# A hybrid decoder step on one Trainium2 core: the mixer one tile at a time, and decode attention alone in later slots

## The chip, the cores and the metric

The kernel runs on one core of one Trainium2 chip. The metric is the device time of one execution in microseconds; before the change it was 2877.15 us, the median of three runs (2869.53 to 2877.79). Smaller is better.

## The reference, cut to what matters

One layer is computed for two groups of tokens with the same weights: a prompt of 512 tokens (four tiles of 128, numbered 0 to 3) and a sample of 8 sequences with 4 new tokens each (32 rows, tile 4, called PT), which see 4096 past tokens in a paged cache. All is float32.

```
h = rms_norm(x); proj = h @ w_in                 # 1024 -> 13 blocks of 512 columns
o_a = stick_breaking_attention(qa, ka, va)       # prompt: keys up to the own tile; sample: 32 pages of 128 keys per sequence
o_b = retention(qb, kb, vb, state)               # prompt: state carried from tile to tile; sample: 8 states loaded and stored
y_b = (rms_norm(o_b) * silu(gb)) @ w_b_up
merged = sigmoid(ga) * (o_a @ w_a_up) + sigmoid(gb_pre) * y_b
x = x + merged @ w_out
h2 = rms_norm(x)                                 # experts: 8 heads, top 16 of 16384 for each token and head
x = x + sum_k softmax(top)_k * gelu(u_tab[e_k] . h2) * v_tab[e_k]
y = x + sigmoid(rms_norm(x) @ w_ple_gate) * (p_emb @ w_ple)
```

Each tile thus reads all of w_in, w_a_up, w_b_up, w_out and the expert query weights, and each head of a tile gathers 16 rows of u_tab and 16 of v_tab (4 KB each) for each of its 128 tokens.

## The kernel before, in words

**Two streams of work.** The expert part is cut into 34 slots, one for each head of each prompt tile, and two for the sample (32 rows by 4 heads fill a slot). A slot is 16 gathers from u_tab into 16 ring buffers, 16 products on VectorE (L1917, in `dve_dots`), the gelu weights (`dve_weights`, whose third instruction is L1930, so that its start marks the slot), 16 gathers from v_tab into the same buffers, and 64 matmuls on TensorE (L1998, in `pe_weigh`); slot i+2's top-k runs two slots ahead. GpSimd issues all gathers (L2009) and, once a block of slots, the h2 rows of the next tile (L2006). A buffer is gathered into for slot i+1 only when `pe_weigh` has read it for slot i.

The rest (the mixer) runs in the background of the slots. It is cut into groups of tiles and stages: N norm, Q the projections qa, ka, va, A prompt attention, D decode attention, R projections and rotation for retention, T retention, G the output gate, M the merge, O the output projection and h2, K the expert queries and scores; then L, the last gate with the embeddings, for each tile. `when(q, stage, unit)` gives each step of each stage a place on the axis of slots, by fixed costs in `STAGE_COST`; each engine has a written-out order in which `Background.until(s)` emits the mixer steps that are due before the part of the slot that comes next. So TensorE, VectorE and ScalarE each execute one list in order, in which slot work and mixer steps alternate, and a wait of one holds up the other.

**Groups before.** `GROUPS = [[0], [1, PT], [2, 3]]`. Group 0 runs ahead of the slots; group 1, with the sample and decode attention, is placed at slots -0.5 to 5.9; group 2 at 6.02 to 15.9. From slot 16 on only the gates (L) remain. The slots of the sample are 16 and 17, between tile 1 and tile 2.

**Weights.** `load_weights` (L439) loads halves of 1024 KB on SyncE's queue into three buffers, in the order of `W_ORDER`: 44 halves for each group (26 of w_in, 4 of w_b_up, 2 of w_a_up, 4 of w_out, 8 of peer_w_q). Each half is used by all tiles of the group. `project` (L453) is 8 matmuls of 128x512 outputs for a tile, `sample_parts` (L463) the same for the 32 rows of the sample in four column groups, which ScalarE copies (`keep_parts`) and TensorE adds (L478).

**Decode attention.** 64 units, four pages of keys and four of values each (256 KB a page). SyncE reads the page number (L2030) and issues the page's DMA (L2035) in the order of `load_cache`; keys and values have two buffers of four pages each. TensorE turns the keys (L749), ScalarE copies them (L1211), TensorE makes the scores (L760), and, some units later, weighs the values (L812). In group 1 it stands between A and R, so all of R to K of tile 1 and of the sample comes after it.

**Retention of the sample** (L919, L927, in T): for each of the 8 sequences a state of 512 KB is loaded, used, updated on VectorE (L1712) and stored, with two buffers. SyncE waits for each update and each store in its order (L2069, L2072).

**Start of the slots.** GpSimd waits for group 0's K on all engines, then loads the h2 rows and waits for the index of slots 0 (`pool.wait_ge(idx_put, 2)`) before the first gather; VectorE begins the first top-k when the mixer's steps up to -0.9 are done.

## Time and profile before

| | before |
|---|---|
| median of three runs | 2877.15 us |
| profiled execution | 2866.99 us |
| its span | 2865.0 us |
| TensorE busy | 1831.4 us, 64% |
| VectorE busy | 1312.3 us, 46% |
| GpSimd busy | 1227.7 us, 43% |
| ScalarE busy | 493.1 us, 17% |
| moved by DMA | 896.09 MB, mean 313 GB/s |
| mean granted TensorE clock | 0.79 |

Busy shares are means over stages that have different limits. The share of the 16 DMA engines is a mean of the time that packets took; where two queues both have work it can come out a little over 1, and its highest value in a long stretch (1.03) is read as full. GB/s times microseconds gives the bytes of a stretch. The span leaves about 2 us of the execution's own time outside. The granted clock has two levels, 1.2 and 2.4 GHz; 0.79 is a mean of 0.5 and 1.

### The profile page before, as it was taken

How to read it: one execution, taken by the hardware profiler on the slowest of the kernel's cores; microseconds unless marked ns; L12 is line 12 of the kernel's file. 1: busy time of each engine (PE TensorE's matmuls, PEld its weight loads, DVE VectorE, ACT ScalarE, POOL GpSimd, SP SyncE). 2: the span in 40 equal slices, each digit the busy share in tenths (PEclk: the TensorE clock that was granted, in tenths of full speed). 3: DMA queues.
4: the chain of work that ended last, by engine and by line, in shares of the span. 5: the costliest groups of instructions: out<-in, count | busy, mean ns of one | idle time of the engine just before them, and what ended most of it. 6: DMA issues, size and time to landing. Idle time of an engine off the chain costs nothing.

```text
span 2865.0 us, 32111 instructions
## 1 busy us (share of the span) xinstructions
PE 1831.4 (64%) x10812; PEld 932.5 (33%) x10812; DVE 1312.3 (46%) x3316; ACT 493.1 (17%) x1044; POOL 1227.7 (43%) x1172
## 2 busy tenths in 40 slices
PE   5985567676667688876756879887626553235334
PEld 2454244444444243235334333335401110001001
DVE  1113432222222344242557655455557767667753
ACT  2111234333333012011122021011001110001001
POOL 0003431021012142222645655457487767777772
PEclk8997788788888678888978989999857766567666
DMA  5777688899799876777876989899999999999994
GB/s 180 263 248 226 255 295 290 260 315 339 241 310 348 292 274 250 293 248 254 284 280 233 362 300 361 338 343 352 365 364 402 409 373 394 357 410 410 409 408 176
DMA packets 328694, 896.09 MB, mean 313 GB/s; under 512 B 34194, under 2 KB 43571, under 8 KB 328403
## 3 DMA queue, kind: packets, MB, share of 16 engines
q0 software_dynamic: 160512, 580.99, 54.1%
q1 hardware_dynamic: 165762, 307.14, 31.5%
q10 hardware_dynamic: 2256, 5.90, 0.5%
q8 instruction: 88, 1.44, 0.2%
q14 instruction: 76, 0.61, 0.1%
HBM read 878.70 MB, written 15.20 MB: 312 GB/s over the span
## 4 chain that ended last, share of the span: by engine, by line
PE 25%; POOL 17%; DMA 16%; SPq 12%; issue 10%; DVE 6%; ACT 2%; DVEq 0%; ACTq 0%; POOLq 0%
POOL arena L2009 17%; PE ps L453 10%; SPq L2030 6%; SPq L2035 6%; PE ps L1998 4%; DMA arena<-in_w_in_dram 3%; PE ps L1031 3%; DMA arena<-in_cache_k_dram 3%; DMA arena<-in_peer_w_q_dram 2%; DMA arena<-in_peer_v_dram,arena 2%; DMA arena<-in_peer_u_dram,arena 2%; DVE arena L1917 2%; DMA arena<-in_w_b_up_dram 2%; PE ps L749 1%; PE ps L706 1%
## 5 line engine op out<-in xcount | busy, mean ns | idle before, releaser
L2009 POOL DMA_INDIRECT arena<-in_peer_u_dram,arena x544 | 577.7, 1062 | 900.1 <-PE ps L1998 734.6
L2009 POOL DMA_INDIRECT arena<-in_peer_v_dram,arena x544 | 608.3, 1118 | 446.4 <-DVE arena L1917 280.8
L1917 DVE CUSTOM_DVE_ANT_0 arena<-arena 128x1024 f32<-128x1024 f32 x544 | 654.2, 1222 | 284.5 <-DMA arena<-in_peer_u_dram,arena 270.7
L1998 PE MATMUL ps<-arena 128*32 128x512 f32 x2176 | 353.3, 785 | 486.4 <-DMA arena<-in_peer_v_dram,arena 390.7
L453 PE MATMUL ps<-arena 128*128 128x512 f32 x1152 | 551.6, 634 | 92.0 <-DMA arena<-in_w_in_dram 42.7
L453 PEld LDWEIGHTS ps<-arena 128*128 128x128 f32 x1152 | 227.1, 203 | 403.7 <-issue 294.7
L1998 PEld LDWEIGHTS ps<-arena 128*32 128x32 f32 x2176 | 75.9, 131 | 715.9 <-issue 614.1
L749 PE MATMUL ps<-arena 128*128 128x128 f32 x1024 | 187.6, 345 | 140.9 <-DMA arena<-in_cache_k_dram 124.4
L749 PEld LDWEIGHTS ps<-arena 128*128 128x128 f32 x1024 | 146.8, 175 | 203.6 <-DMA arena<-in_cache_k_dram 158.0
L1211 ACT ACTIVATE arena<-ps 128x512 f32<-128x512 f32 x256 | 145.4, 596 | 297.1 <-PE ps L749 296.7
L1031 PE MATMUL ps<-arena 128*128 128x128 f32 (+2 forms) x768 | 143.5, 343 | 49.4 <-DMA arena<-in_peer_w_q_dram 49.4
L2006 POOL DMA_DIRECT2D arena<-h_for_experts x80 | 41.5, 534 | 244.5 <-DVE arena L348 244.5
L1031 PEld LDWEIGHTS ps<-arena 128*128 128x128 f32 x768 | 123.1, 207 | 65.5 <-DMA arena<-in_peer_w_q_dram 51.9
L812 PE MATMUL ps<-arena 128*32 128x512 f32 x512 | 83.8, 731 | 55.4 <-DMA arena<-in_cache_v_dram 55.4
L760 PE MATMUL ps<-arena 128*32 128x128 f32 x2048 | 84.6, 317 | 0.2 <-ACT arena L1211 0.2
L640 PE MATMUL ps<-arena 128*128 128x128 f32 (+1 forms) x280 | 46.2, 313 | 51.7 <-DVE arena L1466 30.9
L1809 DVE COPY arena<-ps 128x128 f32<-128x128 f32 x64 | 17.0, 288 | 130.7 <-PE ps L1012 130.7
L1074 PE MATMUL ps<-arena 128*128 128x512 f32 (+1 forms) x160 | 72.2, 605 | 0.0
L760 PEld LDWEIGHTS ps<-arena 128*32 128x32 f32 x2048 | 63.5, 128 | 18.0 <-ACT arena L1211 10.1
L698 PE MATMUL ps<-arena 64*128 64x128 f32 (+1 forms) x112 | 29.8, 447 | 57.9 <-DVE arena L1515 51.2
L640 PEld LDWEIGHTS ps<-arena 128*128 128x128 f32 (+1 forms) x280 | 37.1, 168 | 77.6 <-issue 44.2
L1590 DVE COPY arena<-ps 128x1 f32<-128x1 f32 x16 | 2.5, 159 | 129.3 <-PE ps L786 129.3
(219 smaller groups left out, 1747.7 us busy)
## 6 DMA issues: line engine op xcount, KB each, us to landing
arena<-in_w_in_dram SPq DMA_DIRECT2D x78, 1024.0 KB, 7.4
arena<-in_cache_k_dram SPq DMA_DIRECT2D x256, 256.0 KB
arena<-in_cache_v_dram SPq DMA_DIRECT2D x256, 256.0 KB, 3.6
arena<-in_peer_w_q_dram SPq DMA_DIRECT2D x24, 1024.0 KB, 8.6
arena<-in_w_b_up_dram SPq DMA_DIRECT2D x12, 1024.0 KB, 10.1
arena<-in_w_out_dram SPq DMA_DIRECT2D x12, 1024.0 KB, 7.1
arena<-h_for_experts POOLq DMA_DIRECT2D x80, 128.0 KB, 9.5
arena<-in_peer_u_dram,arena POOLq DMA_INDIRECT x544, 9.8
```

Source lines behind the costliest of these rows:

```text
L453: last = pe.matmul(bank[0:rows(t), :], x[:, c, g.at(t)], weight(pe, g.no, name, c), start=(c == 0), stop=(c == nd - 1))
L640: last = pe.transpose(bank[:, k * P:k * P + n], src[0:n, k * P:(k + 1) * P], ident[0:n, 0:n])
L749: last = pe.transpose(ps[:, hp % 2, k * P:(k + 1) * P], KP[i % 2][:, k, hp * P:(hp + 1) * P], ident)
L760: last = pe.matmul(ps[32 * k:32 * k + 32, 2, r * P:(r + 1) * P], Qb[:, p // 2 % 2, hp, :], KPT[:, r % 2, hp, k * P:(k + 1) * P], start=(hp ...
L812: last = pe.matmul(ps[32 * k:32 * k + 32, 3, :], AdT[:, r, 32 * k:32 * k + 32], VP[i % 2][:, k, :], start=(m == 0 and r == 0 and k > 0), s ...
L1031: last = pe.matmul(bank[:, 0:g.width], w[:, (nb % 4) * P:(nb % 4 + 1) * P], a["hT2"][:, c, :], start=(c == 0), stop=(c == DC - 1))
L1211: act.activation(KPT[:, i % 2, hp, :], ps[:, hp % 2, :], ACT.Copy).then_inc(keys_kept, 1)
L1917: dve.tensor_tensor_reduce(ring[j], ring[j], HREP[:, g, :], 1.0, 0.0, ALU.mult, ALU.add, A16[:, p, 4 * g + a:4 * g + a + 1]).then_inc(u_us ...
L1998: last = pe.matmul(ps[32 * g:32 * g + 32, V_SUM + n, :], DG[:, p, 4 * g + a, :], ring[4 * a + g][:, n * 512:(n + 1) * 512], start=(first_o ...
L2009: pool.indirect_dma_start(ring[j], None, table, bass.IndirectOffsetOnAxis(ap=IDX[:, i % 2, 4 * g + a:4 * g + a + 1], axis=0)).then_inc(row ...
L2030: return sp.value_load(table[0:1, at:at + 1], min_val=0, max_val=ins["cache_k"].shape[1] - 1)
L2035: sp.dma_start(dst[:, k, :], pages[bass.ds(page(u // 4, u % 4, k), 1)].rearrange("a p d -> p (a d)")).then_inc(landed, 16)
```

## The change

The mixer's groups become `[[0], [1], [2], [3, PT]]` and a fifth group without tiles, in which only D, M, O and K of the sample are left. Group 1 stands at slots -0.5 to 5.45, group 2 at 5.55 to 10.95, group 3 at 11.05 to 17.95, D at 18.05 to 28.9, the sample's M (only its two w_a_up blocks), O and K at 28.95 to 29.95. The gates of all tiles move to slots 30.1 to 33.9. The sample's two expert slots move from 16 and 17 to 32 and 33.

Each group loads its own weights: four times 44 halves, and 14 more (2 of w_a_up, 4 of w_out, 8 of peer_w_q) for the fifth. The sample's partial merge goes to DRAM in group 3 and comes back after D (`sample_merge`). The sub-keys and the gain row of the norm are loaded five times in place of three.

The stages' steps are lagged: each engine's step of a stage is placed a fraction of a unit, or one to three units, after the step that it depends on, while before the engines' steps of a unit had one place. Attention of a tile is two steps of 4 heads or four of 2 heads, and its outputs trail the scores by two steps; turning a unit's keys is split in two halves; the carry of decode attention moves from bank 5 to bank 4 with waits of its own; evacuations of turned tiles and of the expert scores move from VectorE to ScalarE. At the start, the first top-k runs when the first scores exist, in the middle of group 0's K, and GpSimd waits only for the stored h2.

```diff
-GROUPS = [Group(0, [0], 0, 0, 4), Group(1, [1], 1, 1, 4), Group(2, [2, 3], 0, 3, 1)]
-BLOCKS = [(0, range(0, 8)), (1, range(8, 16)), (PT, range(16, 18)), (2, range(18, 26)), (3, range(26, 34))]
+for items_, late_, heads_ in (([0], [0], 4), ([1], [1], 4), ([2], [2], 2), ([3, PT], [3], 2), ([], [PT], 2)):
+    GROUPS.append(Group(len(GROUPS), items_, late_, heads_, list(GROUPS)))
+BLOCKS = [(0, range(0, 8)), (1, range(8, 16)), (2, range(16, 24)), (3, range(24, 32)), (PT, range(32, 34))]
...
-STAGE_COST = {"N": (3.0, lambda g: g.n), "Q": (8.0, lambda g: 3 * g.n + 1), "A": (12.0, lambda g: g.steps + 1),
-              "D": (5.5, lambda g: 78 if g.sample else 0), "R": (8.0, lambda g: 4 * g.n + 1),
...
-GATE_SLOT = {0: (18.02, 20.0), 1: (20.1, 22.0), PT: (22.1, 24.0), 2: (27.1, 30.0), 3: (33.7, 33.9)}
-GROUP_SLOT = {0: (-2.0, -1.0), 1: (-0.5, 5.9), 2: (6.02, 15.9)}
+STAGE_UNITS = {"N": (3.0, lambda g: g.n + 1), "Q": (8.0, lambda g: len(g.order(3)) + 4), "A": (6.0, lambda g: g.steps + 4),
+               "R": (8.0, lambda g: len(g.order(4)) + 4), "T": (2.5, lambda g: RH + 12 * g.sample + 3),
+               "G": (8.0, lambda g: len(g.order(2)) + 4), "M": (6.0, lambda g: 8 + 6 * g.sample + 3 if g.n else 5),
+               "O": (6.0, lambda g: 7), "K": (3.5, lambda g: 2 * PEER_H + 3), "D": (5.5, lambda g: 80)}
...
+GATE_SLOT = {0: (30.1, 31.0), 1: (31.0, 32.0), 2: (32.0, 32.9), 3: (32.9, 33.5), PT: (33.7, 33.9)}
+PARTS_OF_TIME = [([(0, s) for s in "NQARTGMOK"], -2.0, -1.0), ([(1, s) for s in "NQARTGMOK"], -0.5, 5.45),
+                 ([(2, s) for s in "NQARTGMOK"], 5.55, 10.95), ([(3, s) for s in "NQARTGMOK"], 11.05, 17.95),
+                 ([(4, "D")], 18.05, 28.9), ([(4, s) for s in "MOK"], 28.95, 29.95)]
...
+            for x in range(g.steps + 3):
+                yield when(q, "A", x)
...
+                if x < g.steps:
+                    scores(x)
+                yield when(q, "A", x + 0.4)
+                if 0 <= x - 2 < g.steps:
+                    outputs(x - 2)
+                if 0 <= x - 1 < g.steps:
+                    suffixes(x - 1)
...
                 if u + 1 < 4 * PERIODS:
-                    turn_keys(u + 1)
+                    turn_keys(u + 1, 0)
...
+                if u + 1 < 4 * PERIODS:
+                    yield when(g.no, "D", u + 1.5)
+                    turn_keys(u + 1, 1)
...
                     if g.sample:
+                        drained(q, "R", "pe", "act", "dve")
+                        load_state(0)
+                        load_state(1)
...
+                drained(3, "K", "pe", "act", "dve")
+                sp.dma_start(table, ins["page_table"].rearrange("b n -> (b n)").rearrange("(a n) -> a n", a=1)).then_inc(table_in, 16)
+                sp.wait_ge(xd_stored, 16 * PT)
+                sp.wait_ge(table_in, 16)
+                load_cache()
...
-                for who in ("pe", "act", "dve"):
-                    past(pool, who, 0, "K")
-                pool.wait_ge(xd_stored, 16 * GROUPS[0].n)
-                pool.wait_ge(h2_stored, 16 * GROUPS[0].n)
-                load_h_rows(pool, 0, 0)
+                pool.wait_ge(h2_stored, 16)
+                for g in range(4):
+                    load_h_rows(pool, 0, g)
                 pool.wait_ge(idx_put, 2)
...
-                mixer.until(-0.9)
-                dve_topk(dve, 0)
-                dve_topk(dve, 1)
-                mixer.until(-0.3)
+                mixer.until(when(0, "K", 5))
+                dve_topk(dve, 0)
+                mixer.until(when(0, "K", 8))
+                dve_topk(dve, 1)
+                mixer.until(-0.9)
```

## Rows read from the trace of the kernel before

**Rows 1.** The page, part 3: packets, MB, share of 16 engines' span.
```profile
q0 software_dynamic: 160512, 580.99, 54.1%
q1 hardware_dynamic: 165762, 307.14, 31.5%
```

**Rows 2.** Busy time by stretch; last three columns: granted clock, DMA share, GB/s.
```profile
0.00:245.00 245.00, 193.70 (x718) 111.02 (x718) 36.47 (x88) 38.73 (x86) 0.27 (x5) 0.92 0.64 215
245.00:350.00 105.00, 51.44 (x240) 24.48 (x240) 53.73 (x147) 22.15 (x43) 55.99 (x48) 0.69 0.86 291
350.00:970.00 620.00, 418.76 (x4200) 267.35 (x4200) 170.60 (x446) 206.85 (x404) 99.24 (x96) 0.79 0.87 293
970.00:1350.00 380.00, 302.69 (x1402) 150.05 (x1398) 136.50 (x325) 51.15 (x122) 112.39 (x96) 0.84 0.75 269
1350.00:1580.00 230.00, 149.13 (x702) 86.61 (x703) 135.67 (x344) 51.44 (x81) 121.94 (x110) 0.82 0.77 269
1580.00:2057.00 477.00, 384.28 (x1638) 193.68 (x1636) 253.69 (x657) 56.31 (x136) 258.64 (x243) 0.91 0.93 345
2057.00:2644.00 587.00, 245.10 (x1452) 74.00 (x1452) 406.54 (x1026) 54.27 (x139) 445.42 (x442) 0.67 1.02 389
2644.00:2811.00 167.00, 51.14 (x352) 12.35 (x352) 113.17 (x274) 4.13 (x17) 127.69 (x130) 0.61 1.03 409
2811.00:2865.00 54.00, 35.20 (x114) 12.98 (x114) 5.94 (x14) 8.05 (x17) 6.12 (x7) 0.72 0.26 100
```

**Rows 3.** VectorE in order of time: starts of slots 0, 6, 16 and 33.
```profile
350.38 0.17 DVE L1930 TENSOR_TENSOR arena<-arena 128x16 f32<-128x16 f32 x1
1350.53 0.18 DVE L1930 TENSOR_TENSOR arena<-arena 128x16 f32<-128x16 f32 x1
2057.19 0.17 DVE L1930 TENSOR_TENSOR arena<-arena 128x16 f32<-128x16 f32 x1
2811.03 0.18 DVE L1930 TENSOR_TENSOR arena<-arena 128x16 f32<-128x16 f32 x1
```

**Rows 4.** SyncE's queue in order of time, during decode attention.
```profile
505.51 3.63 SPq L2035 DMA_DIRECT2D arena<-in_cache_k_dram  x4
509.91 3.63 SPq L2035 DMA_DIRECT2D arena<-in_cache_v_dram  x4
```

**Rows 5.** Busy time in the stretch of decode attention and in the state loop; columns as above.
```profile
366.00:970.00 604.00, 407.61 (x4125) 262.42 (x4123) 159.79 (x403) 203.70 (x396) 95.27 (x92) 0.79 0.88 299
1040.00:1095.00 55.00, 42.11 (x171) 25.03 (x169) 21.84 (x54) 4.06 (x17) 1.98 (x2) 0.59 0.51 177
```

**Rows 6.** Who waited for whom, GpSimd, 1351 to 2057 us: total, times, longest.
```profile
POOL arena L2009 <- PE ps L1998: 222.3, 25, 26.9
```

**Rows 7.** Waits of TensorE, 1351 to 1580 us.
```profile
PE ps L698 <- DVE arena L1515: 41.5, 9, 18.3
```

**Rows 8.** The page, part 6: DMA issues, count, KB each, median us to landing.
```profile
arena<-in_w_in_dram SPq DMA_DIRECT2D x78, 1024.0 KB, 7.4
arena<-in_peer_u_dram,arena POOLq DMA_INDIRECT x544, 9.8
```

**Rows 9.** VectorE and GpSimd in order of time: first expert score, last score, first gather.
```profile
201.29 0.29 DVE L1809 COPY arena<-ps 128x128 f32<-128x128 f32 x1 [7.02 <-PE ps L1012]
243.94 0.29 DVE L1809 COPY arena<-ps 128x128 f32<-128x128 f32 x1 [0.34 <-PE ps L1012]
254.69 0.99 POOL L2009 DMA_INDIRECT arena<-in_peer_u_dram,arena  x1 [7.57 <-ACT arena L1974]
```

**Rows 10.** Busy time of two slots with a gate and one without.
```profile
2157.00:2198.00 41.00, 30.94 (x144) 11.52 (x144) 30.97 (x79) 7.91 (x20) 31.86 (x31) 0.84 1.03 409
2241.00:2284.00 43.00, 31.23 (x143) 11.93 (x144) 31.22 (x79) 7.91 (x20) 33.26 (x33) 0.79 1.03 409
2198.00:2241.00 43.00, 15.73 (x99) 3.74 (x98) 32.06 (x82) 5.41 (x9) 32.95 (x34) 0.53 1.02 398
```

More of the change, by code:

```diff
@@ L106, with __init__ @@
 class Group:
[L109 to L115 removed]
+    def __init__(self, no, items, late, heads, earlier):
+        self.no, self.items, self.late = no, items, late
+        self.tile = items[0] if items else None
+        self.sample = PT in items
+        self.n = len(items)
+        self.n0 = sum(e.n for e in earlier)
+        self.l0 = sum(len(e.late) for e in earlier)
+        self.width = sum(rows(t) for t in items)
         self.heads = heads
[L117 removed]
+        self.steps = H // heads if items else 0
+        self.h0 = sum(e.steps for e in earlier)
+        self.keys = range(self.tile + 1) if items else range(0)
+        self.zw = heads * P * len(self.keys)
     def at(self, t):
@@ L686, in pe_attention @@
             score, suffix, out = plan[q, "A"]
-            keys, hb, off = range(g.tiles[-1] + 1), g.heads, OFF[q]
+            hb = g.heads
             if q == 0:
@@ L702, in suffixes @@
[L702 to L712 removed]
+                            hd, lo, at = h * hb + k, 64 * odd, (j * (hb // 2) + k // 2) * P
@@ L724, in outputs @@
-                filled(last, out[h])
-            yield when(q, "A", 0)
-            order, use, part, after, turn = plan[q, "Q"]
-            wait_free(pe, *turn, *use.values())
-            scores(0)
-            for h in range(g.steps):
-                yield when(q, "A", h)
-                if h:
-                    outputs(h - 1)
-                if h + 1 < g.steps:
-                    scores(h + 1)
-                suffixes(h)
-            yield when(q, "A", g.steps)
-            outputs(g.steps - 1)
+                    lo, at = 64 * (hd % 2), k // 2 * P
@@ L868, in pe_rope @@
-            for m in range(m, len(at)):
-                turn_back(m)
+            pr, turn = plan[q, "R"]
+            items = pr.turned(2)
+            for n in range(len(pr.order) + 3):
+                yield when(q, "R", n)
+                if n < len(pr.order):
+                    pe_product(pe, g, pr, n, lambda name: (a["hT"], DC), a.get("PARTS4"))
+                for m, (place, c, t) in enumerate(items):
+                    if place + 2 == n:
+                        pe.wait_ge(r_rot, 2 * g.n0 + m + 1)
+                        turn_tile(pe, a[("QR", "KB")[c]][:, g.items.index(t), :], rows(t), turn[m], RH)
@@ L891, in pe_retention @@
[L891 to L900 removed]
+            sc, ob, st, own = plan[q, "T"]
@@ L901, in pe_retention @@
+            for x in range(RH + 1):
+                yield when(q, "T", x)
+                if x == 0:
+                    wait_free(pe, *plan[q, "R"][1], *plan[q, "R"][0].use.values())
+                if x < RH:
+                    bank = pe_claims(pe, sc[x])
+                    cs = g.at(g.tile)
+                    filled(pe.matmul(bank[:, 0:P], a["KBT"][:, x, cs], a["QBT"][:, x, cs], start=True, stop=True), sc[x])
+                if x:
+                    outputs(x - 1)
             if not g.sample:
@@ L971, in pe_output @@
+            if -1 in pr.parts_at:
+                yield when(q, "M", 0)
+                pe_parts(pe, g, pr, 0, source, slice(0, NS))
+            for n in range(len(pr.order)):
+                yield when(q, "M", begins(pr, n))
+                if g.n and n == 1:
+                    wait_free(pe, *plan[q, "G"][1])
+                pe_product(pe, g, pr, n, source, a.get("PARTS7"), cs=None if g.n else slice(0, NS))
         def pe_output(pe, g):
-            q, a = g.no, AREA[g.no]
-            turned, order, use, part, after, turned2 = plan[q, "O"]
+            q, a, t = g.no, AREA[g.no], g.late[0]
```

1547 lines of the change are left out of this document (781 added, 766 removed).

## The prediction

> **What bounds the kernel now.** I read the page's DMA part first, then busy time by stretch, cut where slots begin, then the waits inside the stretches. The page: gathers (q0) move 580.99 MB in 54.1% of the span, loads on SyncE's queue (q1) 307.14 MB in 31.5% [rows 1]; with 0.3% for the rest that is 0.864 x 2865 = 2475 us of work for the 16 DMA engines (q1: 2.94 us a MB, q0: 2.67). No compute engine comes near it over the whole. By stretch [rows 2] the share of DMA is 0.64 before the slots, 0.86 up to slot 0, 0.87 in decode attention, 0.75 in the rest of group 1, 0.77 and 0.93 in group 2, then 1.02 and 1.03. 1.03 is full: 4 slots take 167 us there, 41.8 each, at 409 GB/s. Slots 0, 6, 16 and 33 begin at 350, 1351, 2057 and 2811 us [rows 3]: six slots cost 1000 us, ten 707, seventeen 754.
>
> So I keep one account: work plus free capacity, divided by 1.03, is the time. Free capacity of a stretch is its length times (1.03 - share): 96, 18, 99, 106, 60, 48, 6, 0 and 42 us in the order of rows 2, together 475, and (2477 + 475)/1.03 = 2866. The early part and the tail (96 and 42) hang on chains without slots beside them; 337 lie between.
>
> Why the 337 are free: in decode attention SyncE issues four pages in 4.40 us (start to start) [rows 4], so 512 pages need 563 us of the 604 the stage lasts; issue is the limit, at share 0.88 [rows 5]. In the state loop the share is 0.51 [rows 5]. In group 2 gathers wait 222 us for TensorE to read the buffers [rows 6], and TensorE in turn for VectorE's steps of attention, up to 18 us at a time [rows 7]. One late step in an in-order list holds the slot's matmuls, and after about 16 gathers (8.4 MB, 21 us at 409 GB/s) the queue runs dry.
>
> **The change, part by part.**
>
> *Added loads.* Weights go from 3 x 44 = 132 halves (78 of them w_in [rows 8]) to 4 x 44 + 14 = 190: 58 x 1.049 MB = 60.8 MB. Two sub-key tables, two gain rows and the sample's merge there and back are about 3.6 MB. 64.4 MB at 2.70 us a MB (0.93/345, slots 9 to 15 [rows 2]) is 174, at 2.94 [rows 1] 189; I take 2.75, nearer the mixed stretch in which they will lie: 177 us of work. Nothing hides this where DMA is full.
>
> *Decode attention moved to slots 18 to 29.* Its 134.2 MB cost 2.94 a MB now (0.88/299 [rows 5]); beside gathers they should cost between 2.70 and 2.94. I take 2.80: -19. The 184 MB of gathers of these slots cost 2.52 now (1.03/409) and will share the engines: up to 2.70, I take +31. Net +12 us, bounds -32 and +33. Issue no longer limits: 563 us of SyncE in about 865. TensorE has 408 us of decode [rows 5] and 12.8 a slot (51.14/4 [rows 2]), 550 of 865. So the stretch is full: 134.2 x 2.80 + 184 x 2.69 = 871 of work, and I leave 20 us free for in-order waits (now 99). SyncE's DMAs for the unit stand behind waits on the turned keys and used values as before, with 13 us a unit against 8.8 of issue.
>
> *Tiles 1 to 3.* Each has 44 halves and 5.5 to 7 slots. A tile costs TensorE about 194 us (group 0 alone, at clock 0.92 [rows 2]); with 5.5 slots x 12.8 that is 264 of about 395 us, 67%, where slots 9 to 15 ran at 81% busy and share 0.93. DMA has more to do per us of TensorE, and the lags take the VectorE waits of attention out. Free capacity now: 106 in tile 1 with the sample, 60 and 48 in group 2. I take 45 for tiles 1 and 2, and 55 for tile 3 with the sample, whose state loop keeps its eight round trips (a quarter slot is planned for them; at share 0.51 and some 100 us they alone leave 50). The bounds: 60 together, if only the state loop is left, and 214, as now.
>
> *The sample's M, O and K in slot 29.* 14 halves behind the drained decode stage, then a chain through all engines; now this lies in slot 5. 20 us free, bounds 5 and 50.
>
> *Gates in slots 30 to 33.* A slot with a gate costs 41 and 43 us, one without 43 [rows 10]: two full slots were planned for a gate, now one. TensorE's 31 us a slot still fit. 10 us free, bounds 0 and 30. The tail keeps 42: the last gate is now that of 32 rows instead of 128, but its chain is as long.
>
> *The start.* The first expert score exists at 201.3 us and the last at 243.9; the first gather is issued at 254.7 [rows 9]. With the top-k in the middle of K it should go out near 225 to 232. K's own loads then share the engines. I take 25 us off the 96; bounds 0 and 35.
>
> *Sum.* Work 2477 + 177 + 12 = 2666. Free 71 + 42 + 45 + 55 + 20 + 20 + 10 = 263 (the 18 of the stretch before slot 0 are in the tiles' 45). 2929/1.03 = 2844, and 2 outside the span: 2846 for a profiled execution that now takes 2867. That one lies 10 under the median, so **2856 us** for the median, 0.7% less. In words: 189 us of new work against 212 of free capacity used up. It is a small difference of two large terms, and the sign hangs on the second.
>
> A rule bears on tiles 1 to 3. Gathers land in 9.8 us and a half in 7.4 [rows 8], though a half alone would take 2.6 at 409 GB/s: the two queues hold each other up. The Trainium skill (DMA: Bandwidth & Descriptors, Queues, rings and completion order) says that each DMA engine takes turns between the queue rows that have work. By it a tile's 46 MB would flow at no less than half of 409, in 226 us, which fits in its 395, so that gathers can't starve TensorE of weights, and the sum stands; the trace agrees as far as a median of 7.4 us with up to three halves in flight goes. If instead a half had to wait behind 16 gathers, 21 us, three buffers would give 3.1 MB in 21 us, some 150 GB/s, 310 us a tile, and little of TensorE's slack would be left: that is rival A.
>
> **The rivals.**
>
> *A: the tiles' stretch doesn't fill (slower).* TensorE's single list stays the place where slots wait: weight halves, states, and VectorE's slot work between lagged steps. Tiles 1 to 3 have some 470 MB (302 of gathers, 138 of weights, 30 of states, rows of x, keys and stores). My sum gives them (470 x 2.72 + 100)/1.03 = 1338 us, 351 GB/s; the best mixed stretch, slots 9 to 15, ran at 345, group 2 as a whole at 320 (269 and 345 weighted [rows 2]), the rest of group 1 at 269. At 330 GB/s they take 1424, and the median is 2856 + 86 = 2942. It decides from about 342 GB/s down. For it: 351 has not been seen in such a stretch, and the state loop lies in it. Against: TensorE less loaded, and lags at just the waits of rows 7.
>
> *B: decode attention stays at its rate (slower).* If not issue but the chain keys, turn, copy, score sets 299 GB/s [rows 5], 318 MB take 1064 us, 199 more than mine: 3055. Against: the 4.40 us beat of rows 4 shows issue as the limit.
>
> *C: it fills nearly everywhere (faster).* Free 60 for tiles, 10 for decode attention, 15 for slots 29 to 33: 65 us less, 2793.
>
> *D: gain and cost cancel.* Free capacity of 30 to 50 us more than mine: 2868 to 2886. That is no change, since 0.3% (9 us) is about what runs of this kernel tell apart.
>
> **How the numbers follow.** Forecast (2800 to 2868) 0.35, C 0.12, D 0.12, A 0.35, B 0.06. Faster by over 0.3% 0.47, within 0.12, slower 0.41. The range from C to A, 2775 to 2950, leaves out B and the far ends of A and C, some 0.2. The likeliest case's own range is 2800 to 2868.
>
> **What would show it.** Total MB of 960, q1 near 372. First gather at or before 232 us. Slots 18 to 28 at about 79 us each with a share over 1.0 (right) or under 0.95 (B, then SyncE idle and TensorE waiting for ScalarE). Slots 0 to 17 at 74 us on average and 350 GB/s (right) or above 79 (A), with gathers waiting for L1998 over 200 us in total. In slots 30 to 32 the share stays 1.0. The prediction is wrong if q1's work a MB rises above 3.0, if one stage of tile 3 holds the slots for over 100 us, or if the start moves later.

## The result, and the profile after

The changed kernel takes 2932.44 us (median of 4 runs, 2928.41 to 2935.92), the kernel before 2873.34 on the same chip (4 runs, 2857.88 to 2877.79): ratio 1.0215, 95% interval 1.0172 to 1.0258. It is 2% slower, and the interval lies wholly on the slower side; the forecast was 0.7% faster. The profiled execution took 2933.36 us, its span is 2931.5 (before 2865.0).

The DMA queues after, beside [rows 1], and the medians to landing, beside [rows 8] (before, w_in 7.4 and peer_w_q 8.6):
```profile
DMA packets 360764, 960.27 MB, mean 328 GB/s; under 512 B 35250, under 2 KB 44627, under 8 KB 360467
q0 software_dynamic: 160512, 580.99, 52.6%
q1 hardware_dynamic: 197826, 371.24, 35.6%
```
```profile
arena<-in_w_in_dram SPq DMA_DIRECT2D x104, 1024.0 KB, 9.1
arena<-in_peer_w_q_dram SPq DMA_DIRECT2D x40, 1024.0 KB, 12.2
```
The added traffic is as forecast (960 MB, of it 372 on q1). The price is lower than forecast: q1 0.356 x 2931.5 / 371.24 = 2.81 us a MB, q0 2.65. With 0.8% for the other queues the engines' work is 0.890 x 2931.5 = 2609 us, 57 less than I gave. So the traffic didn't cost more than I said; the engines stood free for longer.

Busy time by stretch, the columns of [rows 2]. The stretches are: up to slot 0; slots 0 to 5, 6 to 10, 11 to 17, 18 to 28, 29 and 30, 31 and 32; the tail.
```profile
0.00:299.00 299.00, 219.12 (x832) 124.18 (x833) 71.81 (x184) 51.31 (x124) 47.73 (x52) 0.87 0.78 267
299.00:706.00 407.00, 262.76 (x1338) 131.73 (x1337) 212.61 (x542) 56.44 (x139) 226.20 (x192) 0.84 0.98 372
706.00:1042.00 336.00, 229.47 (x1101) 117.04 (x1100) 182.18 (x456) 51.96 (x115) 178.07 (x167) 0.85 0.96 357
1042.00:1621.00 579.00, 388.09 (x2051) 193.28 (x2051) 282.37 (x702) 88.65 (x206) 265.65 (x240) 0.79 0.86 313
1621.00:2570.00 949.00, 558.07 (x5094) 327.84 (x5093) 397.23 (x1020) 212.84 (x459) 424.63 (x375) 0.72 0.95 348
2570.00:2755.00 185.00, 122.36 (x606) 75.95 (x606) 67.22 (x168) 22.09 (x62) 63.75 (x63) 0.63 0.77 286
2755.00:2856.00 101.00, 62.24 (x270) 23.84 (x270) 57.27 (x133) 19.35 (x41) 72.00 (x75) 0.80 1.00 365
2856.00:2931.00 75.00, 51.83 (x158) 16.41 (x158) 10.20 (x23) 15.66 (x33) 11.10 (x12) 0.82 0.28 109
```
Free capacity, length times (1.03 - share), in that order: 75, 20, 24, 98, 76, 48, 3 and 56 us, together 400. The forecast had 263.

Slots are cut at the third instruction of `dve_weights` (here L1984), as in [rows 3]. VectorE in order of time, slots 18 and 29:
```profile
1620.71 0.17 DVE L1984 TENSOR_TENSOR arena<-arena 128x16 f32<-128x16 f32 x1
2569.91 0.18 DVE L1984 TENSOR_TENSOR arena<-arena 128x16 f32<-128x16 f32 x1
```
Waits from 1621 to 2570 us, decode attention (total, times, longest):
```profile
POOL arena L2061 <- PE ps L2050: 390.1, 25, 44.6
PE ps L843 <- DMA arena<-in_cache_v_dram: 148.5, 40, 7.0
PE ps L772 <- DMA arena<-in_cache_k_dram: 145.4, 38, 13.9
DVE arena L1989 <- ACT arena L2037: 105.8, 11, 30.8
```
TensorE waits 294 us in all for pages of keys and values (L772 turns keys, L843 weighs values), and the gathers (L2061) wait 390 us until TensorE (L2050, `pe_weigh`) has read their buffers. The profile's chain of waits follows the work that ended last back from each step to what released it. A piece of it from 1890 to 1990 us shows how the two hang together (start, us, what):
```profile
1898.77 0.60 ACT arena L1229
1899.42 1.16 PE ps L772 x8
1901.33 0.34 SPq L2103
1901.71 0.28 SPq L2098
1902.18 0.34 issue
...
1915.97 0.34 SPq L2103
1917.07 0.34 SPq L2103
1918.17 5.56 DMA arena<-in_cache_v_dram
1923.77 1.94 PE ps L843 x8
1925.71 3.41 PE ps L2050 x16
```
TensorE turns the keys of one unit (1899), which frees their buffer; SyncE then issues fifteen pages, 1.10 us each with their look-ups, from 1901.33 to 1917.07; the last lands 5.56 us later, TensorE weighs the values, and only then do the next 16 matmuls of `pe_weigh` run and set four gather buffers free. SyncE's queue in order of time shows the beat of [rows 4] again:
```profile
1906.07 3.63 SPq L2103 DMA_DIRECT2D arena<-in_cache_v_dram  x4
1910.47 3.64 SPq L2103 DMA_DIRECT2D arena<-in_cache_k_dram  x4
1914.87 3.63 SPq L2103 DMA_DIRECT2D arena<-in_cache_v_dram  x4
```
Of the chain of the whole stretch, the issue instructions (L2098, L2103) and what is called issue are 10.4 + 8.9 + 9.3 = 29%, pages in flight 35%. In decode attention of the kernel before, the same three parts were 74% of the chain.

Two more places. VectorE waits 284.5 us in all for ScalarE's gelu (L2037), before 72.9; and at slot 30 the chain goes through a load of gate weights. SyncE issues this load only after the sample's K is done on all engines (`drained(4, "K", ...)`), at 2694.29 us, and TensorE's list stands still for it:
```profile
L1989 DVE TENSOR_SCALAR arena<-arena 128x16 f32<-128x16 f32 x34 | 6.1, 180 | 284.5 <-ACT arena L2037 284.5
```
```profile
2691.18 1.01 PE ps L1027 x4
2694.80 27.39 DMA arena<-in_w_ple_gate_dram
2722.24 3.64 PE ps L2050 x16
```
Slot 30 lasts 124 us (2631 to 2755) at a DMA share of 0.65, and more of it is lost just before. The longest single wait of VectorE for the gelu lies there, behind ScalarE's steps of the sample's K; the gathers wait 57.7 us in it:
```profile
2694.52 0.18 DVE L1989 TENSOR_SCALAR arena<-arena 128x16 f32<-128x16 f32 x1 [62.89 <-ACT arena L2037]
```

### The profile page after: what moved, and what is told of

Its sections match the earlier page's. It is cut to its first block, busy times and chain, and to the rows that moved or that the text cites. A ratio compares the mean times of both kernels' runs of the same rounds, so it can differ in the third digit from the quotient of the medians.

```text
span 2931.5 us, 33585 instructions
## 1 busy us (share of the span) xinstructions
PE 1893.9 (65%) x11444; PEld 1010.3 (34%) x11444; DVE 1280.9 (44%) x3220; ACT 518.3 (18%) x1179; POOL 1289.1 (44%) x1172
## 3 DMA queue, kind: packets, MB, share of 16 engines
q1 hardware_dynamic: 197826, 371.24, 35.6%
## 4 chain that ended last, share of the span: by engine, by line
DMA 27%; PE 25%; SPq 6%; DVE 5%; POOL 5%; issue 4%; ACT 2%; DVEq 0%; ACTq 0%; POOLq 0%
DMA arena<-in_cache_v_dram 9%; PE ps L451 6%; POOL arena L2061 4%; PE ps L1040 4%; PE ps L2050 4%; SPq L2098 3%; DMA arena<-in_peer_w_q_dram 3%; DMA arena<-in_w_in_dram 3%; SPq L2103 3%; DMA arena<-in_peer_u_dram,arena 3%; PE ps L772 2%; PE ps L1085 2%; DMA arena<-in_cache_k_dram 2%; DMA arena<-in_w_out_dram 2%; PE ps L843 2%
## 5 line engine op out<-in xcount | busy, mean ns | idle before, releaser
L2061 POOL DMA_INDIRECT arena<-in_peer_u_dram,arena x544 | 628.5, 1155 | 1177.6 <-PE ps L2050 1008.4
L2061 POOL DMA_INDIRECT arena<-in_peer_v_dram,arena x544 | 619.9, 1139 | 211.8 <-issue 161.9
L451 PE MATMUL ps<-arena 128*128 128x512 f32 x1152 | 569.4, 650 | 159.5 <-DMA arena<-in_w_in_dram 65.7
L451 PEld LDWEIGHTS ps<-arena 128*128 128x128 f32 x1152 | 232.6, 209 | 481.2 <-issue 322.1
L2050 PE MATMUL ps<-arena 128*32 128x512 f32 x2176 | 314.2, 705 | 67.1 <-DMA arena<-in_peer_v_dram,arena 31.0
L772 PE MATMUL ps<-arena 128*128 128x128 f32 x1024 | 193.3, 350 | 193.3 <-DMA arena<-in_cache_k_dram 145.4
L1040 PE MATMUL ps<-arena 128*128 128x128 f32 (+1 forms) x1280 | 206.4, 324 | 101.3 <-DMA arena<-in_peer_w_q_dram 101.3
L772 PEld LDWEIGHTS ps<-arena 128*128 128x128 f32 x1024 | 153.2, 180 | 281.1 <-DMA arena<-in_cache_k_dram 157.7
L1040 PEld LDWEIGHTS ps<-arena 128*128 128x128 f32 x1280 | 195.1, 240 | 116.0 <-DMA arena<-in_peer_w_q_dram 103.8
L843 PE MATMUL ps<-arena 128*32 128x512 f32 x512 | 99.7, 863 | 148.5 <-DMA arena<-in_cache_v_dram 148.5
L2050 PEld LDWEIGHTS ps<-arena 128*32 128x32 f32 x2176 | 69.1, 124 | 236.9 <-issue 196.2
L1989 DVE TENSOR_SCALAR arena<-arena 128x16 f32<-128x16 f32 x34 | 6.1, 180 | 284.5 <-ACT arena L2037 284.5
L666 PE MATMUL ps<-arena 128*128 128x128 f32 (+1 forms) x280 | 44.3, 303 | 102.9 <-DVE arena L1525 68.7
L783 PE MATMUL ps<-arena 128*32 128x128 f32 x2048 | 95.1, 345 | 1.8 <-issue 1.1
L783 PEld LDWEIGHTS ps<-arena 128*32 128x32 f32 x2048 | 70.3, 139 | 19.9 <-issue 10.3
L843 PEld LDWEIGHTS ps<-arena 128*32 128x32 f32 x512 | 12.9, 128 | 168.9 <-DMA arena<-in_cache_v_dram 158.8
L1461 ACT ACTIVATE arena<-ps 128x128 f32<-128x128 f32 (+1 forms) x80 | 20.9, 261 | 260.6 <-PE ps L1040 260.4
```

The source lines that it names most:

```text
L451: last = pe.matmul(bank[0:rows(t), :], x[:, c, cs], weight(pe, g.no, name, c), start=(c == 0), stop=(c == nd - 1))
L772: last = pe.transpose(ps[:, hp % 2, k * P:(k + 1) * P], KP[i % 2][:, k, hp * P:(hp + 1) * P], ident)
L783: last = pe.matmul(ps[32 * k:32 * k + 32, 2, r * P:(r + 1) * P], Qb[:, p // 2 % 2, hp, :], KPT[:, r % 2, hp, k * P:(k + 1) * P], start=(hp ...
L843: last = pe.matmul(ps[32 * k:32 * k + 32, 3, :], AdT[:, r, 32 * k:32 * k + 32], VP[i % 2][:, k, :], start=(m == 0 and r == 0 and k > 0), s ...
L1040: last = pe.matmul(bank[:, 0:n], w[:, (nb % 4) * P:(nb % 4 + 1) * P], a["hT2"][:, c, :], start=(c == 0), stop=(c == DC - 1))
L2050: last = pe.matmul(ps[32 * g:32 * g + 32, V_SUM + n, :], DG[:, p, 4 * g + a, :], ring[4 * a + g][:, n * 512:(n + 1) * 512], start=(first_o ...
```

## The experiments

All edits are to the changed kernel, unless the kernel before is named. Ratios are to the kernel before, run beside it. The expectations name three theories of the lost time: P, that the pages come too late (issue on SyncE, two buffers); L, that short steps of the slots stand behind mixer steps in the in-order lists; and B, that the added bytes alone set the time.

This table has the us that each stretch took in the profiled execution, by VectorE's starts of slots ("6-11" runs from the start of slot 6 to that of slot 11). In gelu_first, weigh_early, both mended kernels and two of the kernels before, the instruction that marks a slot's start was itself moved 0.15 slot forward in its list, so their cuts lie a little earlier in the work:
```
                  start  0-6  6-11 11-18 18-29 29-31 31-33 tail
before              350 1000   357   449   488    84    83   54
after               299  407   337   578   949   186   101   75
gelu_first          296  404   329   569   942   182   103   76
weigh_spread        295  423   407   607   953   179   104   75
weigh_early         296  412   327   568   948   201    99   68
one_dma             300  403   349   577   895   184   102   74
pages_small         297  407   344   578   762   180   103   75
one_small           299  406   341   578   642   185   102   74
early_look          299  409   344   580   938   184   100   76
values_act          301  409   340   578   906   183   100   75
gates_early         293  406   344   577   947   172   115   47
w2_small            296  392   302   573   945   181   102   76
no_state_trips      297  407   339   561   948   182   102   75
mended              299  402   335   571   929   175   131   48
mended_act          293  405   335   570   904   176   129   49
before_gelu_first   324 1020   350   452   493    84    83   52
before_values_act   348 1083   361   451   493    83    83   51
before_act_gelu     323 1108   346   457   490    84    83   51
```

**Issue and bytes of decode attention: one_dma, pages_small, one_small.** One DMA for four consecutive pages instead of four with looked-up numbers, so that the sample attends to other pages than the reference's:
```diff
-                    for k in range(4): ... pages[bass.ds(page(u // 4, u % 4, k), 1)] ...
+                    sp.dma_start(dst, pages[4 * u:4 * u + 4].rearrange("a p d -> p a d")).then_inc(landed, 64)
```


> The changed kernel with each unit's four pages loaded by one DMA of 1 MB from consecutive pages, without a look into the page table (so the sample attends to other pages than the reference's); bytes as before, 128 DMAs in place of 512. Theory P (SyncE's 1.1 us a page and the late issue hold TensorE): TensorE's waits for pages (294 us in slots 18 to 28) fall by half or more and the stretch from 949 to 880 or less, the median to 2850 to 2875. Theory B: waits may fall, the stretch stays 930 to 950. Theory L: between, 10 to 30 us shorter.

Only 32 of the 512 columns of each page, four DMAs as before:
```diff
-                        load_pages("cache_k", u, KP[u % 2], keys_in[u % 2])
+                        load_pages("cache_k", u, KP[u % 2][:, :, 0:32], keys_in[u % 2])
```


> The changed kernel with only the first 32 of 512 columns of each cache page loaded (the rest of the key and value buffers is left as it was, so decode attention computes on other data); the same 512 DMAs and page look-ups, 126 MB less. Theory B (bytes set slots 18 to 28 at 2.8 us a MB over 1.03): the stretch of 949 us falls by 300 or more, to 600 to 650. Theory P (issue beat of 8.8 us a unit, 563 us in all, inside a list that has to wait): falls to 700 to 780. Theory L alone: 800 or more.

Both edits together:

> The changed kernel with one DMA for a unit's four pages and only 32 of 512 columns of them (decode attention computes on other data): neither the issue beat nor the bytes of the cache are left, the chain of turn, copy, scores and weights is. With small pages alone slots 18 to 28 took 762 us, with one DMA alone 895, as it is 949. If issue and bytes act one on top of the other: 762 - 54 = 708. If with small pages the issue beat was the whole limit: 600 or less (gathers alone are 460). If the chain on TensorE and ScalarE is the floor: 740 or more.

Measured: one_dma 2874.64 us, ratio 1.0006 (0.9989 to 1.0023); pages_small 2747.62 and one_small 2629.17, one run each. These two compute with buffers that were only partly loaded. Decode attention of the three, busy time by stretch, in this order, each from the kernel named:
```profile
1630.00:2525.00 895.00, 550.46 (x5093) 323.77 (x5092) 398.07 (x1019) 211.90 (x459) 436.75 (x373) 0.72 0.98 369
```
```profile
1626.00:2388.00 762.00, 507.07 (x5096) 301.12 (x5095) 396.71 (x1021) 210.04 (x459) 413.52 (x373) 0.78 0.78 268
```
```profile
1624.00:2266.00 642.00, 463.68 (x5094) 278.59 (x5092) 396.70 (x1020) 207.57 (x459) 421.56 (x371) 0.85 0.91 317
```
The stretch took, with whole pages, 949 with 512 issues and 895 with 128; with 32 columns, 762 and 642. The single DMA gains 54 us here, though SyncE needs only 563 of 949, and 120 with small pages. The 126 MB taken away give 187 us with 512 issues, 1.5 us a MB, and 253 us with 128, 2.0 a MB; the mean price is 2.81. So the stretch isn't bound by bytes alone, at a share of 0.95, and a part of what the bytes free goes to the issue as long as that stays. The DMA rows say the same: from the changed kernel to pages_small the work falls by 308 us (0.95 x 949 to 0.78 x 762), and free capacity rises from 76 to 190.

The 54 us have two parts: free capacity falls from 76 to 45 us, and the work from 902 to 877 us (0.98 x 895) for the same 330 MB, a slightly lower price of a MB where one DMA takes consecutive pages. In all, the single DMA takes back 2.1% of the time (1.0215 to 1.0006), all that was lost. That doesn't make it the only cause, since other losses can be had back as well (below); its own share is the 54 us. What a single DMA would be worth on the kernel before was not run.

**SyncE's work ahead of the wait: early_look.** The four page numbers are looked up before SyncE waits for the buffer, not after:
```diff
+                        found = [page(u // 4, u % 4, k) for k in range(4)]
                         if u >= 2:
                             sp.wait_ge(keys_turned, HP * (u - 1))
-                        load_pages("cache_k", u, KP[u % 2], keys_in[u % 2])
+                        load_pages("cache_k", found, KP[u % 2], keys_in[u % 2])
```


> The changed kernel, with the four page numbers of a unit read into registers ahead of the wait for a free buffer, so that only four DMA issues stand behind the wait; result and bytes as before. Theory P, latency form (pages leave late after the buffer is free): TensorE's page waits fall from 294 by 60 us or more, the stretch of slots 18 to 28 from 949 to 915 to 930, the median to 2900 to 2915. Theory P, rate form (8.8 us a unit of SyncE's time is the limit inside bursts): no change beyond 8 us, as the sum of look-ups and issues is the same. Theory B: no change.

Measured 2923.47 us, ratio 1.0151 (1.0111 to 1.0191), an interval that overlaps the changed kernel's; the stretch 938, 11 us shorter. That is close to what the rate form allows (8 us), less than the latency form asks, and hardly more than the runs tell apart.

**Two queues for the pages: values_act.** The value pages are looked up and issued by ScalarE, inside its list of decode steps and one unit earlier than SyncE did; SyncE keeps the keys:
```diff
+                if 2 <= u - 6 < 4 * PERIODS:
+                    values(u - 6)        # act.value_load and act.dma_start, four pages
```


> The changed kernel with the value pages looked up and issued on ScalarE's DMA queue, one unit earlier than SyncE did, and only the keys on SyncE; result and bytes as the reference's. Slots 18 to 28 took 949 us with 512 issues on SyncE and 895 with 128 (one_dma). Theory P in its rate form: SyncE's beat is halved to 4.4 us a unit, so most of those 54 us come back with the right result: 900 to 915, median 2885 to 2900. Rival: ScalarE's issues (some 1.1 us each, 256 of them) delay its key copies, on which TensorE waits: 940 to 980, median 2925 to 2965.

Measured 2895.14 us, ratio 1.0084 (1.0058 to 1.0109), the stretch 906. So the real pages with the real look-ups gain 43 us, where one_dma gained 54, once the issue is shared: the other order of pages in one_dma isn't needed for such a gain. What of the 43 comes of the shared issue time and what of the one unit's lead isn't separated; early_look, which shortens only the delay behind the wait, gave 11. The waits of this kernel in the stretch:
```profile
POOL arena L2077 <- PE ps L2066: 375.9, 29, 35.7
PE ps L772 <- DMA arena<-in_cache_k_dram: 237.6, 52, 9.0
```
TensorE's wait for values fell from 148.5 to 45.9 us, that for keys rose from 145 to 238: 284 together instead of 294. So the gain doesn't show in the total of TensorE's waits, but in the gathers' (390 to 376) and in a busy time that is 26 us shorter (532 for 558), at a granted clock of 0.75 instead of 0.72.

**ScalarE's gelu ahead of mixer steps: gelu_first.** The gelu of slot i is emitted before the mixer steps of the last 0.15 slot:
```diff
-                    mixer.until(i)
+                    mixer.until(i - 0.15)
                     act_gelu(act, i)
```
and the same before `dve_weights`.

> The changed kernel with ScalarE's gelu step of slot i, and VectorE's weights of slot i, placed 0.15 slot earlier in their lists than the mixer steps around them; all work is the same. Theory L (the slot's short steps stand behind mixer steps in the in-order lists; VectorE waits 284 us for the gelu exponential where it waited 73 before the change): that wait falls below 150 us in total and the time by 50 to 100 us, to 2830 to 2880. Theory P (the two-buffer supply of cache pages holds slots 18 to 28) and theory B (the added bytes are all) both: the wait may fall, the time stays within 10 us of 2932.

Measured 2905.87 us, ratio 1.0118 (1.0085 to 1.0151). VectorE's wait for the gelu fell from 284.5 to 194.0 us, and the time by 27 us, spread over slots 0 to 29, about half of the least that theory L expected. (Whether the 27 come of this wait is taken up with before_gelu_first.)
```profile
DVE arena L1989 <- ACT arena L2037: 194.0, 34, 52.5
```

**Where `pe_weigh` stands: weigh_spread and weigh_early.** Its four parts spread over 0.6 of a slot (the turn of the slot's index on TensorE and its copy on ScalarE also move, from 0.5 to 0.75 and 0.8), or (with gelu_first) drawn together:
```diff
-                        mixer.until(i + 0.1 + 0.1 * a)
+                        mixer.until(i + 0.1 + (0.2 if i < 30 else 0.1) * a)   # weigh_spread
+                        mixer.until(i - 0.05 + 0.05 * a)                      # weigh_early
```


> The changed kernel with the four groups of the slot's matmuls on TensorE placed at 0.1, 0.3, 0.5 and 0.7 of the slot in place of 0.1 to 0.4 (slots 0 to 29), and the index turn after them. Theory L: at most 1.5 decode units stand between two groups in place of 4.4, gathers wait less for TensorE (390 us in slots 18 to 28), that stretch of 949 us gets 40 to 80 us shorter, the median 2860 to 2900. Theory B: no change beyond 10 us. Theory P: 10 to 30 us shorter at most, as page waits remain.

> As gelu_first (ScalarE's gelu and VectorE's weights 0.15 slot earlier in their lists, 2906 us), and TensorE's four groups of slot matmuls at -0.05, 0, 0.05 and 0.1 of the slot in place of 0.1 to 0.4. Theory L (the place of the slot's steps in the in-order lists decides when gathers may go): GpSimd's wait for TensorE falls from 989 us to under 750 and the median to 2840 to 2880, with a gain in every stretch from slot 0 to 29. Rival (the lists cost what they cost, the work only trades places): 2895 to 2915. A loss would say that the row buffers of v are not full yet at that point.

Measured 3052.36 us, ratio 1.0628 (1.0591 to 1.0664), and 2921.34, 1.0149 (1.0118 to 1.0180). Spreading doesn't shorten the decode stretch (953) and lengthens every tile, slots 6 to 10 most (337 to 407). Drawing together nearly halves the gathers' wait for TensorE (989 us in gelu_first, 545), and yet it is no faster than gelu_first: 15 us slower by the medians, 0.3% by the ratios, whose intervals overlap. The wait only changed its name. The gathers now wait 474 us until VectorE's products have read their buffers, 56 in gelu_first, and TensorE waits 61 us for gathered v rows, 23 in gelu_first. So the length of a wait is no measure of what it costs. In weigh_spread the gathers wait 1246 us for TensorE, and VectorE 1106 for the gathers:
```profile
POOL arena L2061 <- PE ps L2050: 1246.1, 103, 36.4
DVE arena L1971 <- DMA arena<-in_peer_u_dram,arena: 1106.5, 359, 31.7
```
I take that for the cause (the last buffers come free late, so the next slot's products start late), but no run isolates it. The moved index copy isn't it: GpSimd waits for ScalarE only once, for 24.7 us, ahead of slot 0.

**The end: gates_early.** The last prompt gate ends before slot 33 instead of after it:
```diff
-GATE_SLOT = {0: (30.1, 31.0), 1: (31.0, 32.0), 2: (32.0, 32.9), 3: (32.9, 33.5), PT: (33.7, 33.9)}
+GATE_SLOT = {0: (30.5, 31.1), 1: (31.1, 31.8), 2: (31.8, 32.4), 3: (32.4, 32.95), PT: (33.7, 33.9)}
```


> The changed kernel with the gates of tiles 0 to 3 at slots 30.5, 31.1, 31.8 and 32.4 to 32.95 in place of 30.1, 31.0, 32.0 and 32.9 to 33.5; the sample's stays at 33.7. Theory: the tail after the start of slot 33 is 75 us and not 54, because tile 3's gate and the sample's both lie in it. It falls to 50 to 58 and the median by 15 to 20 us, 2912 to 2917, and slot 30 (124 us) loses part of its 27 us wait for the gate weights. Rival: the two gates only move into slot 32, which grows by as much: within 8 us of 2932.

Measured 2904.31 us, ratio 1.0108 (1.0053 to 1.0163): 28 us less, more than the 15 to 20 expected. The tail is 47 instead of 75, slots 29 and 30 took 14 less, 31 and 32 14 more; the chain still waits 25 us for the gate weights.

**Tile 2's weights: w2_small.** 32 of 512 columns of tile 2's 44 halves (43 MB less, as many DMAs):
```diff
+                width = 32 if W_HALVES[k][0] == 2 else 512
```


> The changed kernel with only 32 of 512 columns of each weight half of group 2 (tile 2) loaded, so that tile's mixer computes with leftover weights; 43 MB less, in slots 5.5 to 11. Theory B for these slots (share 0.96 to 0.98, so bytes set the time): 43 x 2.7/1.03 = 113 us less in them, 337 falls to about 225, the median to 2820 to 2835. If the lists on TensorE and VectorE hold these slots instead (TensorE busy 229 of 336 us): 30 to 60 us less. The prediction priced the 64 MB that the change adds at 177 us of work, which holds only in the first case.

Measured 2872.93 us, ratio 0.9998 (0.9979 to 1.0016): 60 us less in all, half of the 113 expected by the mean price, and the other case of the expectation. By the table 35 us of it lie in slots 6 to 10 and 15 in slots 0 to 5, where tile 2's first weights are loaded. Slots 6 to 10 of this kernel:
```profile
688.00:990.00 302.00, 227.45 (x1151) 118.15 (x1152) 182.34 (x458) 52.61 (x119) 172.53 (x165) 0.88 0.83 286
```
The share falls from 0.96 to 0.83, so something else than bytes holds the slots now. TensorE's list is the likely one (227 of 302 us busy, 229 of 337 without the edit), but no run shows it.

**Tile 3's states: no_state_trips.** The stores stand behind the last state, and states 2 to 7 aren't loaded anew:
```diff
-                        if b + 2 < DECB:
-                            sp.wait_ge(state_out[b % 2], 16 * (b // 2 + 1))
-                            load_state(b + 2)
```


> The changed kernel with the 8 states of the sample's retention not loaded and stored one by one (two are loaded, the loop goes over them, all are stored at its end; six states' results are left out). The prediction had the round trips alone leave 50 us of free DMA time in slots 11 to 18, which take 579 us. If they do: slots 11 to 18 fall to 520 to 535. If the stretch is held elsewhere (waits for query weights 35 us, for VectorE's steps 42, TensorE's own 388 us): 555 or more.

Measured 2915.15 us (2 runs), ratio 1.0145 (1.0114 to 1.0176). Slots 11 to 17 took 561 instead of 578, a third of the 50 that the prediction had. TensorE no longer waits for states (20.9 us), but 49 us for halves of w_in, 27 before this edit.

**Put together: mended and mended_act.** gelu_first, early_look and gates_early; then gelu_first, gates_early and values_act.

> The changed kernel with gelu_first, gates_early and early_look together; result and bytes as the reference's. Alone they took 27, 28 and 9 us off 2932. If the three losses lie in different places they add up: 2865 to 2875, level with the kernel before (2873). If the slots' steps and the page look-ups share one loss: 2880 to 2895.

> values_act with gelu_first and gates_early (without early_look). Those two and early_look together gave 2888. If the value pages' queue is worth what one_dma showed, 35 to 50 us on top of some 2892: 2845 to 2860, below the kernel before (2873). If ScalarE's list loses what SyncE's gains: 2885 to 2920.

Measured 2887.70 us, ratio 1.0042 (1.0025 to 1.0060), and 2867.44, ratio 0.9987 (0.9969 to 1.0005). The single gains, 27 + 9 + 28 = 64, gave 45, and 27 + 28 + 37 = 92 gave 65, short of the 2845 to 2860 expected of mended_act. Most of what is missing lies in slots 31 and 32, which take 131 and 129 us, where they took 115 in gates_early. With its issue, its gelu and its gates mended, the change is level with the kernel before.

**The same edits on the kernel before: before_gelu_first, before_values_act, before_act_gelu** (the last is the two together).

> The kernel before with the same move of ScalarE's gelu and VectorE's weights 0.15 slot earlier in their lists. There VectorE waited 73 us for the gelu in all, against 284 after the change. If that wait is what gelu_first won back (27 us), the gain is a quarter here: 2865 to 2873 against 2873. If the place of the slot's steps is worth as much in both: 2845.

> The kernel before with the value pages on ScalarE's DMA queue alone. Issue-bound: 2775 to 2805 against 2873; chain-bound: 2845 or more. Beside values_act (37 us won on the changed kernel) it tells how much of the change's hoped-for gain was this one limit.

> The kernel before, with two of the repairs found on the changed one: the value pages on ScalarE's DMA queue one unit earlier, and gelu and weights 0.15 slot earlier. Result as the reference's. If SyncE's 8.8 us a unit set the pace of decode attention in slots 0 to 3 (563 us of issue in a stage of 604), the stage falls to what bytes ask: 185 MB at 2.85 us over 1.03, some 510 us, and the median to 2760 to 2790 (before_gelu_first: 2857). If the chain of turn, copy and score holds it there: 2830 or more.

Measured 2857.51 us, ratio 0.9945 (0.9925 to 0.9964); 2958.99, 1.0296 (1.0267 to 1.0324); 2945.59, 1.0242 (1.0212 to 1.0272). before_gelu_first is the fastest of the kernels here that leave nothing out, mended_act included. Its gain of 16 us isn't where I put it: the wait for the gelu is 68.7 after 72.9. (Slot 0 starts 26 us earlier and slots 0 to 5 take 20 more, in part because the mark itself moved.) So the earlier place wins 16 us where that wait hardly changes, and of the 27 us on the changed kernel perhaps only 11 are a loss that the change brought; no run tells which wait the 16 come from.

Sharing the issue helps the changed kernel by 37 us and costs the other 84, a loss that I had not expected. Waits of before_values_act from 366 to 970 us, where L749 waits for ScalarE 14.6 us in the kernel before:
```profile
ACT arena L1211 <- issue: 219.2, 37, 8.5
PE ps L749 <- ACT arena L1211: 195.0, 59, 8.2
```
And ScalarE in order of time there:
```profile
621.11 3.50 ACTq L1245 DMA_DIRECT2D arena<-in_cache_v_dram  x4
624.71 1.08 ACT L1211 ACTIVATE arena<-ps 128x512 f32<-128x512 f32 x2 [5.92 <-issue]
```
Four pages with their look-ups hold ScalarE for 5.9 us, and the key copies that TensorE waits for stand behind them. Sixty-four units make 379 us of that, beside 204 of ScalarE's own work in a stretch of 604, which leaves no room; in 949 there is.

## Why the prediction was wrong, step by step

- **Sum of bytes and its price.** Right in bytes (960 MB); the work is 2609 us instead of 2666, since a MB on q1 cost 2.81 and one on q0 2.65 over the whole kernel ([rows 1]: 2.94 and 2.67). Taken alone, this would have made the kernel faster than forecast. Two slips: the text says 0.3% for the other queues, while its sum uses the page's 0.8%; and rival D's range, 2868 to 2886, is 12 to 31 us of free capacity over mine, not 30 to 50.
- **The start.** First gather forecast for 225 to 232, measured 227.54; free capacity 75 us, forecast 71. Right.
- **Tiles 1 and 2.** Free 44 us, forecast 45. Right; rates 372 and 357 GB/s. The Trainium skill (DMA: Bandwidth & Descriptors, Queues, rings and completion order) says that each DMA engine takes turns between the queue rows that have work. What I worked out from it, that gathers can't starve the weights, holds as far as the share goes (0.98 and 0.96): halves of w_in land in a median of 11.7 us here and those of peer_w_q in 16.8, below the 21 of a wait behind 16 gathers, though TensorE waits 124 of 743 us for halves. The bound itself isn't confirmed: three halves at half of 409 GB/s would need 15.4 us.
- **Tile 3.** Free 98 us, forecast 55. The state loop, on which I put the 50, is worth 17 by no_state_trips. Slots 0 to 17 took 1322 us all the same, forecast 1338: the 1042 + 579 - 299 us hold 452 MB where I had 470. The gathers are 299 MB of the 302, so most of the difference is on q1, of it some 8 MB in weight halves that lie outside (124 of 132 are loaded in these slots). So the right time is in part luck: more free capacity than forecast and fewer bytes cancel. Rival A didn't come about as a time; its rate, 342 GB/s, did, through tile 3 alone. Nor was my sign for A worth much: gathers wait 502 us for `pe_weigh` in slots 0 to 17, far over its 200, at 73.4 us a slot.
- **Decode attention (the step that failed).** "Issue no longer limits: 563 us of SyncE in about 865 ... So the stretch is full", with 20 us free. It took 949 instead of 865. 76 us were free where I had 20, worth 54 us, and the work is 902 us instead of 871, worth 30: some 12 MB more lie in it than I had (six halves of the sample's M, O and K, h2 rows, early gathers). The average use of SyncE (563 us of 949) was the wrong measure. A unit takes 8.8 us to issue and TensorE's list has the units between its parts of `pe_weigh`, some close behind each other, with two page buffers. In such a burst TensorE runs at SyncE's beat, and as `pe_weigh` stands in the same list, the gathers stop too (390 us). The chain shown above is this burst, and the 54 us by one_dma and 43 by values_act bear it out, though some 24 of the 54 are a lower price of the bytes. Rival B had the effect (a stretch that isn't full) with another cause: of its chain keys, turn, copy, score, TensorE's waits for the copies are only 47.8 us (31 times), and one_small, which leaves that chain as it was, takes 642 us. What holds the stretch at 895 with one DMA I could not settle; the share is 0.98 there and pages in flight are 54% of its chain of waits, so it is closer to full.
- **Slots 29 to 32.** Free 48 + 3 us, forecast 20 + 10. Slot 30 alone takes 124 us at a share of 0.65. Its slot work stands behind the sample's K: VectorE waits 62.9 us for a gelu that ScalarE reaches only then. After that the gate's weights, which SyncE may issue only when K is done, hold the chain for 27 us (the piece shown above); the loads of K's halves hold it for 12.5, 5.0 and 5.1 us before. I had priced the chain of M, O and K, not what stands behind it.
- **The tail.** "The tail keeps 42": it is 56 free and 75 us long, forecast 54. I looked only at the last gate, 32 rows instead of 128; but the gate before it now ends at 33.5, behind slot 33. gates_early gives 28 us back.
- **A term I didn't have.** ScalarE's gelu behind lagged mixer steps. The wait rose by 212 us in total. gelu_first takes 90 of them away and wins 27 us, but the same edit wins 16 on the kernel before, so what this wait is worth stays open. I took the lags for a gain ("take the VectorE waits of attention out") and asked on no other engine what then stands ahead of slot work.

By stretch: -16 in slots 0 to 17, -2 in the start with slots 29 to 32 taken together (51 us free in slots 29 to 32, for 30, hide behind less work elsewhere), +84 in decode attention, +21 in the tail: 87 of the 2931 - 2844. The measured time lies within the stated range and near rival A's 2942, but that is luck: A put the loss into slots 0 to 17, where there was none, and B, which named the right stretch, had the wrong cause and 3055 us. The sign hung on the free capacity, as I wrote; the error was the belief that a stretch with a low average load on each engine fills up. What a run shows of it is the single DMA's 54 of the 84 us in decode attention and the gates' 28 us, more than the tail's 21; the rest is read from the rows.

## What to carry to other kernels

An engine or queue that is half busy on average can still limit where its work comes in bursts with few buffers behind it, and through an in-order list it then holds up work that has nothing to do with it; so compare its rate with that of the burst, not of the stretch. A gain in free capacity is only there if each list (ScalarE's and the queue's too) is read for what now stands ahead of the work that the slots wait for. When bytes are taken away in a stretch that is nearly full, their mean price is the most to expect: here it was half of it, and 0.7 once the issue limit was gone too.

## What the hardware showed that I had not expected

- Bytes taken away gave back less than their mean price of 2.81 us a MB, at shares of 0.95 and 0.96: 187 us for 126 MB of pages (1.5 us a MB) with 512 issues, 253 us (2.0) with 128, and 60 us for 43 MB of weights (1.4). A share near 1 is no proof that bytes alone set the time.
- The granted clock was 0.72 on average in decode attention after and 0.79 before [rows 5], but 0.85 in one_small with the same matmuls. TensorE's waits for pages were 294 us (changed kernel), 243 (one_dma), 159 (pages_small) and 66 (one_small), and the clock 0.72, 0.72, 0.78 and 0.85: where it waits less it also works less of the time at the lower of its two levels (1.2 and 2.4 GHz). PE's busy time of the stretch went with it, 558 us against 464, so TensorE's busy time isn't a fixed load to sum up.
- A page issued by ScalarE costs about what it costs on SyncE (3.50 us for four against 3.63), and with the look-ups stops its computing for 5.9.
